# Convolution's output gate in four pairs of tiles with seven block products each, behind eight plain tiles

## The reference

```
def odd_mixer(h, w_in, conv_w, w_out):
    S = h.shape[1]
    proj = h @ w_in                                 # 1024 x 3072
    b_gate = proj[..., :CONV_DIM]
    c_gate = proj[..., CONV_DIM:2 * CONV_DIM]
    z = c_gate * proj[..., 2 * CONV_DIM:]
    zp = jnp.pad(z, ((0, 0), (CONV_WIDTH - 1, 0), (0, 0)))
    y = zp[:, 0:S] * conv_w[0]
    for tap in range(1, CONV_WIDTH):
        y = y + zp[:, tap:tap + S] * conv_w[tap]
    return (b_gate * y) @ w_out
```

## Time and profile before

| what | value |
|---|---|
| device time, median of 3 runs (lowest to highest) | 2213.42 us (2212.22 to 2215.15) |
| device time of the profiled execution | 2213.02 us |
| span of the profile, first to last instruction | 2211.1 us |
| PE busy | 2196.4 us, 99% of the span, 12112 matmuls |
| DVE busy | 1452.8 us, 66% |
| ACT busy | 977.1 us, 44% |
| mean share of the DMA queue for transfers | 38.9% |

### The profile page before, as it was taken

One profiled execution on the slowest core, in us unless ns is written; L12 is line 12 of the kernel. 1 busy time (PEld: TensorE's weight loads), 2 busy tenths in 40 slices (PEclk: granted clock), 3 DMA queues, 4 the chain that ended last, 5 costly groups with the idle time before them and its releaser, 6 DMA issues.

```text
span 2211.1 us, 31738 instructions
## 1 busy us (share of the span) xinstructions
PE 2196.4 (99%) x12112; PEld 1860.6 (84%) x12112; DVE 1452.8 (66%) x2444; ACT 977.1 (44%) x1680; POOL 14.5 (1%) x14
## 2 busy tenths in 40 slices
PE   9999999999999999999999999999999999999998
PEld 7887888888778888888898888998888888899997
DVE  5866665558656566686665767766755657776775
ACT  5444543434445244475554544443322435444444
POOL 0000000000000000200000000000000000000000
PEclk9999999999999999999999999999999999999999
DMA  5555443245644323464353233333332213233331
GB/s 202 178 180 162 152 122 109 96 132 181 179 142 153 115 96 119 124 190 143 110 166 125 86 106 101 99 104 97 96 95 96 86 48 105 95 97 104 96 110 54
DMA packets 136695, 268.14 MB, mean 121 GB/s; under 512 B 21774, under 2 KB 79932, under 8 KB 136161
## 3 DMA queue, kind: packets, MB, share of 16 engines
q1 hardware_dynamic: 136544, 266.13, 38.9%
HBM read 235.37 MB, written 26.77 MB: 119 GB/s over the span
## 4 chain that ended last, share of the span: by engine, by line
PE 96%; DVE 2%; DMA 1%; ACT 1%; POOL 1%; issue 0%; SPq 0%; DVEq 0%; POOLq 0%; ACTq 0%
PE ps L2119 30%; PE ps L2121 30%; PE ps L2120 29%; PE ps L2147 2%; PE ps L2136 2%; POOL t_UP L2102 1%; DMA far<-t_UP 0%; PE ps L2171 0%; PE ps L2161 0%; PE ps L2159 0%; PE ps L2160 0%; PE ps L2173 0%; PE ps L2172 0%; PE ps L2190 0%; DVE t_Tb L2666 0%
## 5 line engine op out<-in xcount | busy, mean ns | idle before, releaser
L2119 PE MATMUL ps<-t_P0H,t_whi 128*128 128x512 f32 (+1 forms) x1568 | 590.8, 377 | 2.8 <-DVE t_P0L L2483 1.7
L2120 PE MATMUL ps<-t_P0L,t_whi 128*128 128x512 f32 (+1 forms) x1568 | 584.6, 373 | 0.0
L2121 PE MATMUL ps<-t_P0H,t_wlo 128*128 128x512 f32 (+1 forms) x1464 | 553.0, 378 | 0.0
L2438 DVE TENSOR_TENSOR t_wlo<-t_raw,t_whi 128x1024 fp32r<-128x1024 f32 (+2 forms) x289 | 342.2, 1184 | 48.4 <-PE ps L2121 36.2
L2262 ACT ACTIVATE t_whi<-t_raw 128x1024 fp32r<-128x1024 f32 (+2 forms) x295 | 300.6, 1024 | 155.0 <-PE ps L2121 153.4
L2119 PEld LDWEIGHTS ps<-t_P0H,t_whi 128*128 128x128 f32 x1568 | 295.4, 188 | 72.1 <-issue 15.5
L2120 PEld LDWEIGHTS ps<-t_P0L,t_whi 128*128 128x128 f32 x1568 | 295.1, 188 | 56.1 <-issue 1.0
L2121 PEld LDWEIGHTS ps<-t_P0H,t_wlo 128*128 128x128 f32 x1464 | 275.3, 188 | 54.7
L2119 PE MATMUL ps<-t_P1H,t_whi 128*128 128x512 f32 (+1 forms) x548 | 210.1, 383 | 1.6 <-DVE t_P1L L2821 1.0
L2120 PE MATMUL ps<-t_P1L,t_whi 128*128 128x512 f32 (+1 forms) x548 | 208.5, 380 | 0.0
L2121 PE MATMUL ps<-t_P1H,t_wlo 128*128 128x512 f32 (+1 forms) x524 | 201.1, 384 | 0.0
(11 more groups left out here) (348 smaller groups left out, 3877.7 us busy)
## 6 DMA issues: line engine op xcount, KB each, us to landing
t_raw<-in_wts SPq DMA_DIRECT2D x362, 512.0 KB, 3.6
far<-t_Tb SPq DMA_DIRECT2D x26, 384.0 KB, 3.1
far<-t_Tb SPq DMA_DIRECT2D x16, 512.0 KB, 3.7
t_PTX<-far SPq DMA_DIRECT2D x64, 96.0 KB, 3.4
t_raw<-in_wts SPq DMA_DIRECT2D x16, 384.0 KB, 3.1
t_QKV<-far SPq DMA_DIRECT2D x32, 128.0 KB, 3.0
t_raw<-in_wts SPq DMA_DIRECT2D x13, 256.0 KB, 2.9
t_PTX<-far SPq DMA_DIRECT2D x24, 128.0 KB, 2.7
```

What stands on the lines that cost most here:

```text
L2119: e.matmul(s.out, s.sh, s.mh, start=s.first, stop=False, skip_group_check=again)
L2120: e.matmul(s.out, s.sh, s.ml, start=False, stop=False, skip_group_check=again)
L2121: i = e.matmul(s.out, s.sl, s.mh, start=False, stop=s.end, skip_group_check=again)
L2438: e.tensor_tensor(s.dst, s.raw, s.hi.bitcast(F32), ALU.subtract).then_inc(*mark("lo", s.j))
```

## The change

The convolution's stage is rewritten as `conv()`. Of its 24 output tiles, 16 stay plain (c and x for each of the eight `m`), and the eight tiles of the output gate b become four pairs of seven block products. The eight plain tiles c and x of m = 0 to 3 come first. The other eight run beside the pairs: c4, x4 and c5 in pair 0; x5 and c6 in pair 1; x6 and c7 in pair 2; x7 in pair 3. Inside a pair there are three places for them (`places`): a pair with three uses all, a pair with two uses the first and the last, and pair 3 only the last.

The stage needs T1 to T4 of its norm. So the first layer's perceptron now ends with its last eight tiles written out one by one, with `gain 0` and `gain 1` behind tiles 6 and 7, and the `combine` steps stand behind the first seven plain tiles of the convolution. The value y that waits for the gate moves from the `TMP` buffers to the buffer `QKV`, and the squared row of the norm moves from `E3` to `UP`. The gate's two DVE operations now read a `TMP` buffer in place of a PSUM bank.

```diff
-            run(second(7))
+            tread[0] = "product", prods[0] - 1
+            for m in range(8):
+                if m % 2 == 0:
+                    w = Weight(chunk("mlp_w2", l, halves(512 * 7, 4), halves(128 * m, 2)))
+                run(second_tile(7, m, w, m % 2))
+                combine(*{6: ["gain 0"], 7: ["gain 1"]}.get(m, []))
...
-        for base, ev in ((1024, ev_c), (2048, ev_x), (0, ev_b)):
-            w = Weight(chunk("conv_w_in", 0, halves(0), halves(base + 128 * m, 1)))
-            run(gemm_fm(P0, w, parts8(), ev))
...
+        def gate_out(m, t, after):
+            emit("conv_b", m=m, s=t, t=y(m), after=after, row=N.row)
+            split_into(P1, m, t, ("conv_out", m), give=t)
...
+        first = [(g, m) for m in range(4) for g in "cx"]
+        beside = [[("c", 4), ("x", 4), ("c", 5)], [("x", 5), ("c", 6)], [("x", 6), ("c", 7)], [("x", 7)]]
+        places = {3: (0, 1, 2), 2: (0, 2), 1: (2,)}
...
+        plain(5, "low 2", "high 3")
+        u0(0)
+        plain(6, "low 3")
+        low(0, "u0")
+        sums(0)
+        u12(0, 0)
+        plain(7)
+        low(0, "u1", A[0][0])
+        u12(0, 1)
+        next_to(0, 0)
+        low(0, "u2", A[0][1])
+        low(0, "w0", B[0, 0])
+        u3(0)
+
+        def pair_of_tiles(q):
...
+            p = product(bx, u["u0"], 0, "B11", True, xf)
+            s1 = snap(a0, p, af)
+            if q == 0:
+                low(0, "u3")
+            next_to(q, 1)
+            p = product(bz, u["u0"], 4, "B21", True, zf)
+            u["u0"].done(p)
+            c11 = add(a0, z, s1, p)
+            PB.give(bz, c11)
+            low(q, "w1", B.get((q, 1)))
+            u0(q + 1)
+            other(q, 0)
...
+            p = product(bx, u["u1"], 0, "T2", False, [s1])
+            s2 = snap(b0, p, bf)
+            low(q + 1, "u0")
+            p7 = product(bv, u["u2"], 0, "T3", True, vf)
+            next_to(q, 2)
+            sums(q + 1)
+            low(q, "w2", B.get((q, 2)))
+            u12(q + 1, 0)
+            other(q, 1)
+            low(q + 1, "u1", A[q + 1][0] if more else None)
...
+            p = product(bx, u["u3"], 0, "T1", False, [s2])
...
+            s3 = snap(b1, p)
+            c22 = add(b1, v, s3, p7)
+            u3(q + 1)
+            other(q, 2)
+            next_to(q + 1, 0)
+            low(q + 1, "u3")
+            p = product(bx, u["u1"], 4, "B22", False, [s3])
+            u["u1"].done(p)
+            low(q + 1, "w0", B.get((q + 1, 0)))
+            c12 = snap(a1, p)
+            PB.give(bx, c12)
+            u12(q + 1, 1)
...
+            gate_out(2 * q, tA, [c11, c12])
+            p = product(bv, u["u2"], 4, "T4", False, [c22])
+            u["u2"].done(p)
+            c21 = add(b0, v, s2, p)
+            PB.give(bv, c21)
+            low(q + 1, "u2", A[q + 1][1] if more else None)
+            gate_out(2 * q + 1, tB, [c22, c21])
```

More of the change, by code:

```diff
@@ L1617, in cross @@
             if m == 5:
+                tread[0] = "x_values", ids["x_values"]
                 combine("gain 0", "gain 1")
@@ L1628, in schedule @@
     T4R, T4F = T["E3R"], T["E3"]
-    ttok, tsum = [None] * 4, [None] * 4
+    ttok, tsum, tread = [None] * 4, [None] * 4, [None]
     def combine(*work):
@@ L1642, in combine @@
                 emit("combine", t=u.t, of=u.id, x=X[:, k + 4, :], col=gcol(u.gain, k + 4), T=both,
-                     read=("x_values", ids["x_values"]))
+                     read=tread[0])
                 TMP.give(u.t, ("combined", u.id))
@@ L1943, in n1 @@
         norm_tile(m, o, "mix1", P0, sqa)
+        if m > 3:
+            tsum[m - 4] = Rec(gain="mix1", x=o)
     mlp(0, n1)
     row_end()
-    R2 = E3[:, 8, :]
+    R2 = UP[:, 2, 0:512]
     emit("conv_zero", dst=UP[:, 0:2, 0:16])
[L1952 to L1975, removed]
-        for base, ev in ((1024, ev_c), (2048, ev_x), (0, ev_b)):
-            w = Weight(chunk("conv_w_in", 0, halves(0), halves(base + 128 * m, 1)))
-            run(gemm_fm(P0, w, parts8(), ev))
@@ L1980, in schedule @@
+    conv()
     flush()
-    cuts = split_kv(1, [k for _, f in blocks.idle + grouped.idle + turned.idle for k in f])
+    cuts = split_kv(1, [k for _, f in blocks.idle + grouped.idle + turned.idle for k in f] +
+                    ([] if dry else [("product", prods[0] - 1)]))
     for n, _ in enumerate(mixed("conv_w_out", 0, halves(0), 1.0, "xa1", P1)):
@@ L2840, in vector_program @@
         elif s.name == "conv_c":
-            for k in s.free:
-                e.wait_ge(*at(*k))
             if new(("row_squared", 0)):
@@ L2845, in vector_program @@
             e.wait_ge(*at(*s.p))
-            e.tensor_tensor(s.t, s.bank, s.r2, ALU.mult).then_inc(*mark("conv_c", s.id))
+            e.tensor_tensor(s.t, s.bank, s.r2, ALU.mult).then_inc(*mark("conv_c", s.m))
         elif s.name == "conv_x":
@@ L2849, in vector_program @@
                 e.wait_ge(*at("conv_zero"))
-            e.wait_ge(*at("conv_c", s.id))
+            e.wait_ge(*at("conv_c", s.m))
             e.wait_ge(*at(*s.p))
-            e.tensor_tensor(s.z, s.bank, s.t, ALU.mult).then_inc(*mark("conv_x", s.id))
-            e.wait_ge(*at("conv_x", s.id))
+            e.tensor_tensor(s.z, s.bank, s.t, ALU.mult).then_inc(*mark("conv_x", s.m))
+            e.wait_ge(*at("conv_x", s.m))
             (z2, c2), (z1, c1), (z0, c0) = s.taps
-            e.tensor_scalar(s.t, z2, c2, None, ALU.mult, ALU.bypass).then_inc(*mark("tap2", s.id))
-            e.wait_ge(*at("tap2", s.id))
+            e.tensor_scalar(s.t, z2, c2, None, ALU.mult, ALU.bypass).then_inc(*mark("tap2", s.m))
+            e.wait_ge(*at("tap2", s.m))
             e.scalar_tensor_tensor(out=s.t, in0=z1, scalar=c1, in1=s.t, op0=ALU.mult,
-                                   op1=ALU.add).then_inc(*mark("tap1", s.id))
-            e.wait_ge(*at("tap1", s.id))
+                                   op1=ALU.add).then_inc(*mark("tap1", s.m))
+            e.wait_ge(*at("tap1", s.m))
             e.scalar_tensor_tensor(out=s.t, in0=z0, scalar=c0, in1=s.t, op0=ALU.mult,
-                                   op1=ALU.add).then_inc(*mark("tap0", s.id))
+                                   op1=ALU.add).then_inc(*mark("tap0", s.m))
         elif s.name == "conv_b":
-            for k in s.free:
-                e.wait_ge(*at(*k))
             if new(s.row):
                 e.wait_ge(*at(*s.row))
[L2867 to L2871, removed]
+            for k in s.after:
+                e.wait_ge(*at(*k))
+            e.tensor_tensor(s.s, s.s, RB[:, :], ALU.mult).then_inc(*mark("conv_b", s.m))
+            e.wait_ge(*at("conv_b", s.m))
+            e.wait_ge(*at("tap0", s.m))
+            e.tensor_tensor(s.s, s.s, s.t, ALU.mult).then_inc(*mark("conv_out", s.m))
         elif s.name == "final_sums":
```

139 lines of the change are left out of this document (added).

## The result

| | before | changed |
|---|---|---|
| median of 22 runs each (lowest to highest) | 2213.47 us (2212.22 to 2216.16) | 2217.49 us (2214.59 to 2219.73) |
| time of the profiled execution | 2213.02 | 2218.37 |
| span of the profile | 2211.1 | 2216.6 |
| the stage: first matmul of the convolution to the first of `conv_w_out` | 133.94 | 137.86 |

The ratio is 1.0016, with an interval of 1.001 to 1.0022. The changed kernel is 4.0 us slower by the medians; that is under the 0.2% taken as the bound, but both ends of the interval lie above 1. The forecast was 2214.4 us, range 2210.8 to 2218.2.

The account below looks back on a forecast made before the run. PE's matmuls were taken to bound the kernel. The terms -4.8 - 0.4 + 3.9 + 2.3 + 0 made +1.0 us, giving 2214.4 us with the basis adjusted to the median; range 2210.8 to 2218.2.

Parts of the forecast that it names:

- The matmuls: Output gate's 192 matmuls become 336 of 256 columns, gaining 4.8 us; tiles beside the pairs gain 0.4 more.
- Wait A: At tile c4 in pair 0, PE waits 3.9 us for DVE's low part of its weights.
- Wait B: In pair 3, PE waits 2.3 us at T2 for ACT's copy s1, with no tile there to cover it.
- Pairs 1 and 2, start and end of the stage: No PE wait taken in these places; at most 0.5 us at the start and 0.2 at the end.
- Rival 4: DVE falls behind in pairs 1 and 2, a fetch holds ACT in pair 3: stalls of 1.5 us, 2218.4 us; 7%.
- 1 and 2: Rivals: both stalls hidden, 2208.2 us, 9%; only one stall, 2212.1 us without B or 2210.5 without A, 14%.
- The clock: The sum added both stalls at their own length, with no term for a slower PE clock.
- Rival 3: PE's clock falls to half in stall A: 2217.4 us for 6.1 us at the lower level, 2219.4 for 10; 10%.

Follow-up runs that it names:

- A taken away: Changed kernel with the weights of tile c4 made before plain tile 6, two plain tiles sooner, on ACT and DVE; 2212.31 us, ratio 0.9997.
- B taken away: Changed kernel with the gate of tile 5 and the first two `conv_w_out` chunks put behind pair 3's second copy out of PSUM; 2214.08 us, ratio 1.0004.
- both taken away: Changed kernel with both of those edits together, and u2's parts ahead of u1's; 2207.41 us, ratio 0.9976.
- before, held 3.9: Kernel before, with PE held once in the convolution after the b tile of m = 3, until five spare DVE operations end; 2219.26 us, ratio 1.0028.
- before, held 2.4: Kernel before, with PE held once at the same place until three spare DVE operations end; 2217.17 us, ratio 1.0017.
- before, held 1.7: Kernel before, with PE held once at the same place until two spare DVE operations end; 2215.46 us, ratio 1.0009.

## Why the prediction was right in part, and where it failed

The length of the stage gives one account for all eight profiles, the kernel before being the eighth. "Bare" is its 133.94 us for it and those made from it, 128.69 for the changed kernel and its variants:

| profile | stage | over bare | waits | what is left | low stretches |
|---|---|---|---|---|---|
| changed | 137.86 | 9.17 | 3.81 + 2.06 | 3.30 | 2 |
| A taken away | 132.09 | 3.40 | 1.21 + 2.06 | 0.13 | 0 |
| B taken away | 134.15 | 5.46 | 3.81 | 1.65 | 1 |
| both taken away | 128.69 | 0 | 0 | 0 | 0 |
| before, held 3.9 | 139.37 | 5.43 | 3.90 | 1.53 | 1 |
| before, held 2.4 | 138.02 | 4.08 | 2.44 | 1.64 | 1 |
| before, held 1.7 | 135.75 | 1.81 | 1.72 | 0.09 | 0 |

- **The matmuls: right.** Forecast -4.8 and -0.4; the stage without waits is 5.25 us shorter. By the pitches there, 192 x 231.6 - 336 x 118.1 ns = 4.8 us for the gate. The tiles beside the pairs take 228.0 ns, which gives 0.7 rather than 0.4 (the forecast's own figures, 192 x (231.7 - 229), make 0.5), and the plain ones 232.8, which takes 0.2 back.
- **Wait A: right.** 3.81 us for 3.9, ended by c4's low part. DVE's order was counted out to 6.6 us behind the start of pair 0; the rows have 1613.65 + 1.22 against a start near 1608.4, so 6.5.
- **Wait B: right.** 2.06 us for 2.3, by the copy s1, behind ACT's high part of tile 5. The forecast's own count, 5.05 - 2.83, is 2.2; with this and the 0.5 above its sum would have been +0.8 us.
- **Pairs 1 and 2, start and end of the stage: right.** No wait of PE from 1619 to 1684, and none at `conv_w_out`. Rival 4 is out, and so are 1 and 2, which needed a wait to be hidden.
- **The clock: the step that failed.** The sum gave the waits their own length and nothing more. In the profiled run they cost 3.3 us on top, 1.65 each. With it the stage's account is -5.25 + 3.81 + 2.06 + 3.30 = +3.92 us, and the medians show the same (+4.0), where +1.0 was forecast. Rival 3, given 10%, was the one that happened. It was right on the mechanism. Its price was taken from the end of the kernel, 6.1 us at the lower level, and a figure of 10 us; each stretch is 3.4 us. And it named A alone, where B, half as long, brings the clock down too. So it is luck that its 2217.4, for one stretch of 6.1 us, lies 0.1 us from the measured median: two stretches of 3.4 us made it up.

That the time still lies inside the range is owed to the range's upper end, drawn for rival 3, not to the forecast's mechanism. The reason why the rival got so small a chance was that no wait in the trace of before was long enough to show what one does to the clock; that is a reason to put the chance near the middle, not to take it low. The Trainium skill spoke for it ("TensorE: Matmul & The Clock Gate", section "Why this matters for your kernels": an idle stretch between bursts sends the clock back to half), and the traces of the changed kernel and of the holds agree, at 3.81 and 3.90 us. They also show it behind 2.44 and once behind 2.06 us, shorter than the gaps that the section warns of.

Of the 5.5 us between the two profiled executions, 3.92 is the stage. 1.07 had gathered before it, where both kernels run the same matmuls (half of it in the first 11 us), and some 0.5 behind it. I read these as differences between executions: the other variants' stages begin at 1561.7 to 1565.5, three of them sooner than before's 1562.07.

What stays open: why the clock falls behind one wait of 2.06 us and not behind another. In the single profile of each, it fell behind 2.01, 2.06, 2.44, 3.81 (twice) and 3.90 us, and not behind 1.21, 1.72 and another 2.06. Nor did it behind a wait of 1.82 us near the start of the changed kernel (2.05 less a matmul), where its grant is 1.00:

```profile
8.18 0.40 PE L2332 MATMUL ps<-t_P0H,t_wlo 128*128 128x512 f32 x1
10.23 0.50 PE L2330 MATMUL ps<-t_P0H,t_whi 128*128 128x512 f32 x1 [1.65 <-DVE t_P0L L2694]
```

The medians fit this only loosely. The run held 1.7 us is 2.4 us over before where 1.8 was paid in its profile, and two of its ten runs stand at 2217.19; with one fall of 1.6 us in some runs that would come out, but these runs have no timeline here, so it is inferred, not shown. In the same way the changed kernel's shortest runs look like ones with no fall or one. Each run's mean granted clock fits that: it is 0.998 or 0.999 in the five runs below 2216 us and 0.996 or 0.997 in 16 of the other 17, where one fall takes 0.0008.

## What to carry to other kernels

In this kernel, a wait of PE of 2 us or more in the midst of dense matmuls is to be priced at its length plus some 1.6 us, since a stretch at half clock followed six of the seven such waits in these profiles; the shorter ones, up to 1.8 us, cost their length there. So a lead-in that leaves PE a wait may lose more than the arithmetic it introduces saves: here 5.25 us of gain met 5.87 us of waits and 3.30 us of clock, and a few steps moved in the order turned +4.0 into -5.8 us by the medians. When a stage is given a new form, walk each engine's order through its first and its last piece, where neighbours are missing; the middle ones of the four pairs ran without a wait.

## What the runs showed of the hardware

- Where dense matmuls follow, the low stretch has one length, 3.4 us, whether the wait before it was 2.06 or 3.90 us, and whether PE then runs matmuls with 256 or 512 columns. They are 213 and 427 ns apart in it, for 118 and 228 to 233 at full clock.
- It does not begin at the wait. It began 0.3 us ahead of the restart behind the wait of 3.90 us, and 0.1 to 1.1 us after it behind the other five.
- Two matmuls with 256 columns cost 236 ns where one with 512 costs 232, with a weight load for each; halving the columns costs 2% and is no obstacle to seven products for eight, which give back 12.5%.
